# Experts' small products: two groups of four row pairs in every expert instead of three groups

## The chip, the cores and the metric

The kernel runs on one core of one Trainium2 chip. The metric is the time of one execution on the device in microseconds (us), the median of several runs. Engines are named as in the profile: PE is TensorE (PEld its weight loads), ACT is ScalarE, DVE is VectorE, POOL is GpSimd, SP is SyncE, and SPq and POOLq are their DMA queues.

## The reference

One step of a two-layer hybrid trunk over a prompt of 128 tokens and a sample of 1024 tokens, model width 1024, all in float32. Each layer ends with an expert-choice SwiGLU block of 16 experts of width 1024, on which the change bears:

```python
def expert_choice_ffn(h, w_router, w_gate, w_up, w_down):
    B, T, D = h.shape
    cap = EC_CAPACITY * T // N_EXPERTS
    aff = jax.nn.softmax(jnp.einsum('btd,de->bte', h, w_router, preferred_element_type=jnp.float32), axis=-1)
    gate, idx = lax.top_k(aff.swapaxes(1, 2), cap)
    xg = jax.vmap(lambda hb, ib: hb[ib])(h, idx)
    a = jnp.einsum('becd,edf->becf', xg, w_gate)
    u = jnp.einsum('becd,edf->becf', xg, w_up)
    y = jnp.einsum('becf,efd->becd', jax.nn.silu(a) * u, w_down) * gate[..., None].astype(h.dtype)
    return jax.vmap(lambda yb, ib: jnp.zeros((T, D), yb.dtype).at[ib.reshape(-1)].add(yb.reshape(-1, D)))(y, idx)
```

Each expert takes 128 rows of the sample and 16 rows of the prompt. Prompt and sample use the same weights.

## The kernel before, in words

A layer's expert block is `experts` (line 1756 on). Five instruction streams, one for each engine, run side by side and meet at semaphores; the order within each is written out by hand.

The weights come in **chunks** of 128 rows x 1024 columns (512 KB): eight gate chunks (G0 to G7, by k), eight up chunks (U0 to U7) and eight down chunks (D0 to D7) for each expert. `weight_order` (line 1503) lists them: G0, U0, G1, U1, ... G7, U7 of expert e, then D0 to D7 of expert e-1, then the next expert. A chunk n lives in tile n mod 14 of `ffn_w` (`raw_rows`, `RAW_ROOM = 14`).

- SyncE (line 1809 on) loads chunk n when the small products of chunk n-14 are finished:

```python
if n >= RAW_ROOM:
    sp.wait_ge(small_done, 4 * (small[order[n - RAW_ROOM]] + 1))
    sp.dma_start(raw_rows(wall, n), weight_rows(io, l, *chunk)).then_inc(w_in[n % RAW_ROOM], 16)
```

- ScalarE (line 1993) rounds each raw chunk to `w_high`, and VectorE (line 2069) takes the rest as `w_low`; there are `CUT_ROOM = 8` tiles of each, so these two run at most eight chunks ahead of TensorE.
- TensorE multiplies each chunk in `big` (line 1897): three passes (high x high, low x high, high x low) in two halves of 512 columns, into the banks G, U or Y, for the 128 sample rows.
- The 16 prompt rows are multiplied in `small_rows` (line 1919) from the raw chunk itself, without rounding: four products of 16 rows side by side in four column strips of the array, for each k. Of gate and up these are two strips each. Each product counts one on `small_done`, which is what releases the raw tiles.

Where the small products stand in TensorE's order (`k` is the row pair, G and U of one k):

- expert 0: a group for k 0 to 3 after pair 5, and a group for k 4 to 7 after pair 7
- experts 1 to 15: a group for k 0 and 1 after pair 3, a group for k 2 and 3 after pair 5, and a group for k 4 to 7 after pair 7
- the down chunks of expert e-1: a group for k 0 to 3 after D5 and one for k 4 to 7 after D7

In between TensorE also turns things by transposes: h of the expert before after pairs 0 and 1, its prompt part after pair 2, and the gathered tokens of expert e+1 after pairs 4 and 6 (`turn_tokens`). VectorE scales the turned tokens (`set_tokens`, line 2021; the first half behind G6 and the second behind D0), ScalarE rounds them behind D1 (`round_tokens`, line 1985), VectorE cuts them behind D2 (line 2034). Behind D4 ScalarE does the SiLU (lines 1967 to 1972) and VectorE the products with up (`multiply`, lines 2040 and 2044), ahead of D5. GpSimd gathers the tokens of a later expert (line 1816) after `turn_tokens` has freed their buffer, and adds the results back (line 1832).

Of the kernel before, what the change touches and what calls it, by code (L numbers as in the profile page):

```python
# [1516 lines left out]
def raw_rows(wall, n):  # L1517
    return wall[:, (n % RAW_ROOM) * D:(n % RAW_ROOM + 1) * D]
# [237 lines left out]
def experts(nc, io, keep, l, wall):  # L1756
# [7 lines left out]
    with Stage(nc, f"moe{l}") as s:  # L1764
# [86 lines left out]
        def _(pe):  # L1851
            def turn_tokens(e, i):
                if e and i:
                    pe.wait_ge(x_set, NF * e + i)
                elif i == 0:
                    pe.wait_ge(xg_in[e % 2], 16 * (e // 2 + 1))
                    if e >= 2:
                        pe.wait_ge(hpT_done, e - 1)
                    elif e:
                        pe.wait_ge(xp_set, 4)  # L1860
                for k in range(4 * i, 4 * i + 4):
                    mm = nc.tensor.transpose(turned(k, e), xg[e % 2][:, k * P:(k + 1) * P], keep.ident[:])  # L1862
                mm.then_inc(x_turned, 1)

            def turn_prompts(n):
                g, i = divmod(n, 2)
                if n == 0:
                    pe.wait_ge(xgp_in, 16 * (E // PG))
                    pe.wait_ge(x_set, NF)
                else:  # L1870
                    pe.wait_ge(xp_set, n)
                for k in range(4 * i, 4 * i + 4):
                    mm = nc.tensor.transpose(turned(k), xgp[g][:, k * P:(k + 1) * P], keep.ident[:])
                mm.then_inc(xp_turned, 1)

            def turn_h(e, half):
                pe.wait_ge(h_done, e + 1)
                if half:
                    pe.wait_ge(hT_cut, 2 * e + 1)
                for f in range(4):  # L1880
                    mm = nc.tensor.transpose(turn_bank[:, f * P:(f + 1) * P], h[:, (4 * half + f) * P:(4 * half + f + 1) * P], keep.ident[:])
                mm.then_inc(h_turned, 1)

            def turn_hp(e):
                pe.wait_ge(hp_done, e + 1)
                pe.wait_ge(hT_cut, 2 * e + 2)
                for f in range(4):
                    mm = nc.tensor.transpose(turn_bank[:, f * 64:f * 64 + 48], hp[64:112, f * P:(f + 1) * P], keep.ident[64:112, 64:112])
                mm.then_inc(hp_turned, 1)

            def big(bank, stat, e, m, k):
                n = place[e, m, k]
                pe.wait_ge(w_cut, n + 1)
                cut = (w_high[n % CUT_ROOM], w_low[n % CUT_ROOM])
                for i, (a, b) in enumerate(((0, 0), (0, 1), (1, 0))):
                    for half in range(2):
                        mm = nc.tensor.matmul(bank[:, half, :], stat[a][:, k, :], cut[b][:, half * BANK:(half + 1) * BANK],  # L1897
                                              start=k == 0 and i == 0, stop=k == KD - 1 and i == 2)
                mm.then_inc(big_done, 1)

            def small_rows(e, ks, down):
                if not down and ks[0] == 0:
                    pe.wait_ge(xp_set, 4)
                    if e >= 2:
                        pe.wait_ge(yp_done, e - 1)
                if down and ks[0] == 0:
                    pe.wait_ge(hpT_done, e + 1)
                    pe.wait_ge(hp_done, min(e + 2, E))
                    if e == E - 1:
                        pe.wait_ge(yp_done, E - 1)  # L1910
                for k in ks:
                    for q in range(4):
                        if down:
                            n = place[e, "d", k]
                            out, stat, w = small_bank[32 * q:32 * q + CAP_P, 0:256], hpT[:, k // 4, k % 4, :], raw_rows(wall, n)[:, 256 * q:256 * q + 256]
                        else:
                            n = place[e, "gu"[q // 2], k]
                            out, stat, w = small_bank[32 * q:32 * q + CAP_P, :], xpT[:, k, e // PG, CAP_P * (e % PG):CAP_P * (e % PG + 1)], raw_rows(wall, n)[:, BANK * (q % 2):BANK * (q % 2 + 1)]
                        nc.tensor.matmul(out, stat, w, start=k == 0, stop=k == KD - 1, tile_position=(0, 32 * q)).then_inc(small_done, 1)  # L1919

            def down(e):
                if e:
                    pe.wait_ge(ys_done, e)
                pe.wait_ge(hT_cut, 2 * e + 2)
                for k in range(KD):
                    big(Y, (hT_high, hT_low), e, "d", k)
                    if k == 5:
                        small_rows(e, range(0, 4), True)
                small_rows(e, range(4, KD), True)
# [4 lines left out]
            for e in range(E):  # L1934
                pe.wait_ge(x_cut, e + 1)
                if e:
                    pe.wait_ge(h_done, e)
                for k in range(KD):
                    big(G, (xT_high[e % 2], xT_low[e % 2]), e, "g", k)
                    big(U, (xT_high[e % 2], xT_low[e % 2]), e, "u", k)  # L1940
                    if e and k < 2:
                        turn_h(e - 1, k)
                    if e and k == 2:
                        turn_hp(e - 1)
                    if e == 0 and k < 4:
                        turn_prompts(k)
                    if e + 1 < E and k in (4, 6):
                        turn_tokens(e + 1, (k - 4) // 2)
                    if k == 3 and e:
                        small_rows(e, range(0, 2), False)  # L1950
                    if k == 5:
                        small_rows(e, range(2 if e else 0, 4), False)
                small_rows(e, range(4, KD), False)
                if e:
                    down(e - 1)
# [1044 lines left out]
```

## Time and profile before

| What | Value |
|---|---|
| median of 3 runs | 4338.5 us (4337.12 to 4351.47) |
| the profiled execution | 4344.62 us |
| its span, first to last instruction | 4342.8 us |
| TensorE busy over the span | 3623.0 us (83%) |
| VectorE / ScalarE / GpSimd busy | 2370.0 / 1644.5 / 606.4 us |
| mean granted TensorE clock | 0.906 |
| gate and up small products, line 1919 | 2048 records, 237.9 us busy |

The two expert blocks lie at about 1280 to 2080 us and 3490 to 4310 us of the span. Matmuls overlap one another in the records, so the step between two of them is read from their starts, not from their durations. A matmul on plain float32 shows as two records, so a group of 8 small products is "x16" in the timeline and one of 16 is "x32". In a timeline the value in square brackets is the engine's idle time before the row and what ended it.

### The profile page before, as it was taken

The numbers are of one execution on the slowest core, as the hardware profiler recorded it, in microseconds if no ns is written. First come the engines' busy times: TensorE is split into PE (matmuls) and PEld (weight loads), VectorE is DVE, ScalarE is ACT, GpSimd is POOL, SyncE is SP. The second block draws the span as 40 slices with busy tenths as digits, with TensorE's granted clock in tenths as the row PEclk, the third lists the DMA queues.
The fourth block names the chain that finished last, engine by engine and source line by source line (L and its number), as shares of the span: only waits on it lengthen the run. The fifth ranks groups of instructions, "written<-read, shape, count | busy, mean of one in ns | idle before, by whom it ended". The sixth has DMA issues, their size and how long they took to land. (4 is left out here: it accounts for less than half of the span.)

```text
span 4342.8 us, 55242 instructions
## 1 busy us (share of the span) xinstructions
PE 3623.0 (83%) x21964; PEld 2647.4 (61%) x21964; DVE 2370.0 (55%) x3534; ACT 1644.5 (38%) x2480; POOL 606.4 (14%) x472
## 2 busy tenths in 40 slices
PE   3997869797839999999599978419996669999995
PEld 2994524343726666666499956319995446666663
DVE  3233351233477778787412444454555568787874
ACT  2114520000215656565211156524433136565653
POOL 2003110110100001000200000015651000010000
PEclk7998879898969999999799989759997879999997
DMA  4219521411536887887443120352325338878885
GB/s 159 84 61 288 172 73 73 164 53 49 177 147 235 293 296 274 290 291 255 122 118 102 68 89 14 106 148 71 96 71 195 141 142 293 296 274 289 295 284 193
DMA packets 363509, 742.56 MB, mean 171 GB/s; under 512 B 98664, under 2 KB 204279, under 8 KB 362152
## 3 DMA queue, kind: packets, MB, share of 16 engines
q1 hardware_dynamic: 343914, 682.21, 44.9%
q0 software_dynamic: 16720, 56.41, 5.3%
q8 instruction: 175, 2.87, 0.3%
q10 hardware_dynamic: 2618, 0.40, 0.1%
q14 instruction: 82, 0.67, 0.0%
HBM read 633.47 MB, written 106.10 MB: 170 GB/s over the span
## 5 line engine op out<-in xcount | busy, mean ns | idle before, releaser
L2069 DVE TENSOR_TENSOR moe_w_low<-ffn_w,moe_w_high 128x1024 fp32r<-128x1024 f32 x768 | 899.2, 1220 | 97.5 <-ACT moe_w_high L1993 85.3
L1993 ACT ACTIVATE moe_w_high<-ffn_w 128x1024 fp32r<-128x1024 f32 x768 | 778.2, 1053 | 317.0 <-DMA ffn_w<-moe_w_gate 139.3
L1919 PE MATMUL moe_small<-ffn_w,moe_xpT 128*16 128x512 f32 x2048 | 237.9, 594 | 0.0
L1897 PE MATMUL moe_G<-moe_w_high,moe_xT_high 128*128 128x512 f32 x512 | 187.0, 447 | 23.6 <-issue 12.1
L297 PE MATMUL proj_mm<-proj_hT_low,proj_w_high 128*128 128x384 f32 x576 | 193.2, 335 | 0.0
L297 PE MATMUL proj_mm<-proj_hT_high,proj_w_low 128*128 128x384 f32 x576 | 193.1, 335 | 0.0
L297 PE MATMUL proj_mm<-proj_hT_high,proj_w_high 128*128 128x384 f32 x576 | 193.1, 335 | 0.0
L2595 PE MATMUL gdnc_a<-gdnc_T,gdnc_kg 128*128 128x64 f32 (+1 forms) x864 | 102.1, 267 | 89.0 <-ACT gdnc_T L2645 86.8
L297 PE MATMUL proj_mm<-proj_w_high,proj_hT_low 128*128 128x416 f32 (+1 forms) x504 | 176.0, 349 | 0.0
L297 PE MATMUL proj_mm<-proj_w_high,proj_hT_high 128*128 128x416 f32 (+1 forms) x504 | 175.6, 348 | 0.0
L297 PE MATMUL proj_mm<-proj_w_low,proj_hT_high 128*128 128x416 f32 (+1 forms) x504 | 174.8, 347 | 0.0
L1832 POOL DMA_INDIRECT scratch_x<-moe_ys,keep_slot_s x32 | 50.5, 1579 | 877.1 <-DVE moe_ys L2061 877.1
L500 DVE CAST proj_w_high<-proj_w_raw 128x768 fp32r<-128x768 f32 (+1 forms) x60 | 35.0, 583 | 252.1 <-PE proj_mm L297 207.5
L1897 PE MATMUL moe_Y<-moe_w_high,moe_hT_high 128*128 128x512 f32 x512 | 169.8, 413 | 0.0
L1897 PE MATMUL moe_U<-moe_w_high,moe_xT_high 128*128 128x512 f32 x512 | 162.8, 399 | 0.2 <-DVE moe_w_low L2069 0.2
L1897 PE MATMUL moe_G<-moe_w_low,moe_xT_high 128*128 128x512 f32 x512 | 162.8, 399 | 0.0
L1897 PE MATMUL moe_Y<-moe_w_low,moe_hT_high 128*128 128x512 f32 x512 | 162.6, 399 | 0.0
L1897 PE MATMUL moe_Y<-moe_w_high,moe_hT_low 128*128 128x512 f32 x512 | 162.5, 399 | 0.0
L1897 PE MATMUL moe_G<-moe_w_high,moe_xT_low 128*128 128x512 f32 x512 | 162.0, 398 | 0.0
L1897 PE MATMUL moe_U<-moe_w_low,moe_xT_high 128*128 128x512 f32 x512 | 161.7, 397 | 0.0
L1897 PE MATMUL moe_U<-moe_w_high,moe_xT_low 128*128 128x512 f32 x512 | 161.4, 396 | 0.0
L2021 DVE TENSOR_SCALAR moe_xT<-moe_turn,keep_coef 128x128 f32<-128x128 f32 x248 | 84.8, 405 | 125.8 <-PE moe_turn L1862 125.8
(460 smaller groups left out, 7421.9 us busy)
## 6 DMA issues: line engine op xcount, KB each, us to landing
ffn_w<-moe_w_gate SPq DMA_DIRECT2D x256, 512.0 KB, 6.4
ffn_w<-moe_w_up SPq DMA_DIRECT2D x256, 512.0 KB, 7.2
ffn_w<-moe_w_down SPq DMA_DIRECT2D x256, 512.0 KB, 5.6
attnrun_m_w<-w_ada SPq DMA_DIRECT2D x40, 1024.0 KB, 10.7
scratch_conv<-proj_zf POOLq DMA_DIRECT2D x24, 512.0 KB, 2.9
scratch_tm<-proj_tm SPq DMA_DIRECT2D x45, 208.0 KB, 1.9
proj_w_raw<-even_w_in SPq DMA_DIRECT2D x24, 384.0 KB, 4.0
scratch_spec<-filt_res SPq DMA_DIRECT2D x36, 256.0 KB, 2.1
```

The costliest lines, as they stand in the source:

```text
L297: mm = nc.tensor.matmul(out, lhs(a, k), rhs(b, k), start=n == 0, stop=n == len(passes) - 1)
L500: nc.vector.tensor_copy(high, raw).then_inc(w_up, 1)
L1832: nc.gpsimd.indirect_dma_start(out=io["x"][l], out_offset=bass.IndirectOffsetOnAxis(ap=rows, axis=0), in_=src[e % 2][:], in_offset=None, c ...
L1897: mm = nc.tensor.matmul(bank[:, half, :], stat[a][:, k, :], cut[b][:, half * BANK:(half + 1) * BANK], start=k == 0 and i == 0, stop=k == K ...
L1919: nc.tensor.matmul(out, stat, w, start=k == 0, stop=k == KD - 1, tile_position=(0, 32 * q)).then_inc(small_done, 1)
L1993: nc.scalar.activation(w_high[n % CUT_ROOM][:], raw_rows(wall, n), ACT.Copy).then_inc(w_up, 1)
L2021: ins = nc.vector.tensor_scalar(xT[:, k, :], turned(k, e), co[:, 0, k:k + 1], co[:, 1, k:k + 1], ALU.mult, ALU.add)
L2069: nc.vector.tensor_tensor(w_low[n % CUT_ROOM][:], raw_rows(wall, n), w_high[n % CUT_ROOM][:].bitcast(F32), ALU.subtract).then_inc(w_cut, 1)
L2595: mm = nc.tensor.matmul(quad(ba[hg])[later, h, :], kg[n % 3][:, 4 * hg + h, later], earlier(Tm[n % 2][:, 4 * hg + h, :], li, d), start=Tru ...
```

## The change

In experts 1 to 15 of both layers the group for k 0 and 1 after pair 3 goes away, and the group after pair 5 takes k 0 to 3, as in expert 0.

```diff
                     if e + 1 < E and k in (4, 6):
                         turn_tokens(e + 1, (k - 4) // 2)
-                    if k == 3 and e:
-                        small_rows(e, range(0, 2), False)
                     if k == 5:
-                        small_rows(e, range(2 if e else 0, 4), False)
+                        small_rows(e, range(0, 4), False)
                 small_rows(e, range(4, KD), False)
```

On TensorE, behind pair 3 of an expert (`moe_small` is the bank of the small products, `moe_U` and `moe_G` those of up and gate):

```order
 L1897 MATMUL moe_U<-moe_w_low,moe_xT_high 128x512 x2
 L1897 MATMUL moe_U<-moe_w_high,moe_xT_low 128x512 x2
-L1919 MATMUL moe_small<-ffn_w,moe_xpT 16x512 x8
 L1897 MATMUL moe_G<-moe_w_high,moe_xT_high 128x512 x2
 L1897 MATMUL moe_G<-moe_w_low,moe_xT_high 128x512 x2
```

The eight small products of k 0 and 1 are gone from this place; U3 is followed by G4 at once.

On TensorE, behind pair 5 of the same expert:

```order
 L1897 MATMUL moe_U<-moe_w_low,moe_xT_high 128x512 x2
 L1897 MATMUL moe_U<-moe_w_high,moe_xT_low 128x512 x2
-L1919 MATMUL moe_small<-ffn_w,moe_xpT 16x512 x8
+L1919 MATMUL moe_small<-ffn_w,moe_xpT 16x512 x16
 L1897 MATMUL moe_G<-moe_w_high,moe_xT_high 128x512 x2
 L1897 MATMUL moe_G<-moe_w_low,moe_xT_high 128x512 x2
```

They stand here now, ahead of those of k 2 and 3. No other instruction of any engine changes its place, and SyncE's loads and what they wait for are written as before.

## Rows read from the trace of the kernel before

**Rows 1.** Windows in the expert block of layer 0; start:end, length, busy of each engine
```profile
1600.00:1700.00 100.00, 100.00 (x609) 66.98 (x606) 78.70 (x89) 57.28 (x62) 8.55 (x7) 1.00 0.83 288
...
1594.00:1598.00 4.00, 4.00 (x21) 3.11 (x19) 2.53 (x6) 2.59 (x3) 0.00 (x0) 1.00 1.01 408
```

**Rows 2.** Timeline of PE, expert 6 of layer 0; start, length, line, operation
```profile
1589.53 0.63 PE L1897 MATMUL moe_U<-moe_w_high,moe_xT_low 128*128 128x512 f32 x2
1590.09 1.91 PE L1919 MATMUL moe_small<-ffn_w,moe_xpT 128*16 128x512 f32 x16
...
1592.50 0.63 PE L1897 MATMUL moe_G<-moe_w_low,moe_xT_high 128*128 128x512 f32 x2
...
1598.17 1.91 PE L1919 MATMUL moe_small<-ffn_w,moe_xpT 128*16 128x512 f32 x16
...
1605.67 0.63 PE L1897 MATMUL moe_U<-moe_w_high,moe_xT_low 128*128 128x512 f32 x2
1606.23 3.63 PE L1919 MATMUL moe_small<-ffn_w,moe_xpT 128*16 128x512 f32 x32
1609.79 0.73 PE L1897 MATMUL moe_Y<-moe_w_high,moe_hT_high 128*128 128x512 f32 x2
1610.36 0.63 PE L1897 MATMUL moe_Y<-moe_w_low,moe_hT_high 128*128 128x512 f32 x2
```

**Rows 3.** Timeline of PE, expert 0 of layer 1: group, G7, U7, group
```profile
3536.10 3.63 PE L1919 MATMUL moe_small<-ffn_w,moe_xpT 128*16 128x512 f32 x32
...
3543.64 0.73 PE L1897 MATMUL moe_G<-moe_w_high,moe_xT_high 128*128 128x512 f32 x2 [0.47 <-DVE moe_w_low L2069]
...
3545.14 0.63 PE L1897 MATMUL moe_U<-moe_w_high,moe_xT_high 128*128 128x512 f32 x2
...
3546.63 3.63 PE L1919 MATMUL moe_small<-ffn_w,moe_xpT 128*16 128x512 f32 x32
```

**Rows 4.** Timelines of SP, ACT and DVE, the same expert; the loads' landing times
```profile
3537.29 0.35 SPq L1811 DMA_DIRECT2D ffn_w<-moe_w_gate  x1
...
3541.26 1.06 ACT L1993 ACTIVATE moe_w_high<-ffn_w 128x1024 fp32r<-128x1024 f32 x1 [13.69 <-DMA ffn_w<-moe_w_gate]
...
3542.36 3.79 DVE L2069 TENSOR_TENSOR moe_w_low<-ffn_w,moe_w_high 128x1024 fp32r<-128x1024 f32 x3 [5.50 <-ACT moe_w_high L1993]
3546.06 1.36 DVE L2021 TENSOR_SCALAR moe_xT<-moe_turn,keep_coef 128x128 f32<-128x128 f32 x4
...
DMA to landing us min/median/max: 3.4/6.2/12.7
```

**Rows 5.** Timeline of PE, expert 0 of layer 0: its two small groups
```profile
1316.17 3.63 PE L1919 MATMUL moe_small<-ffn_w,moe_xpT 128*16 128x512 f32 x32
...
1327.55 3.63 PE L1919 MATMUL moe_small<-ffn_w,moe_xpT 128*16 128x512 f32 x32
```

**Rows 6.** Timeline of ACT, expert 6 of layer 0: G7, U7, then the tokens
```profile
1594.97 1.06 ACT L1993 ACTIVATE moe_w_high<-ffn_w 128x1024 fp32r<-128x1024 f32 x1 [2.76 <-DMA ffn_w<-moe_w_gate]
1596.24 1.06 ACT L1993 ACTIVATE moe_w_high<-ffn_w 128x1024 fp32r<-128x1024 f32 x1 [0.20 <-DMA ffn_w<-moe_w_up]
...
1604.95 1.06 ACT L1985 ACTIVATE moe_xT_high<-moe_xT 128x1024 fp32r<-128x1024 f32 x1 [5.12 <-DVE moe_xT L2021]
```

**Rows 7.** Timeline of DVE, expert 6 of layer 0: the tokens, and from D5 on
```profile
1603.55 1.37 DVE L2021 TENSOR_SCALAR moe_xT<-moe_turn,keep_coef 128x128 f32<-128x128 f32 x4 [2.17 <-PE moe_turn L1862]
...
1613.51 10.08 DVE L2069 TENSOR_TENSOR moe_w_low<-ffn_w,moe_w_high 128x1024 fp32r<-128x1024 f32 x8
```

**Rows 8.** Timelines of PE and ACT: an early first load, a late second load
```profile
3856.31 1.91 PE L1919 MATMUL moe_small<-ffn_w,moe_xpT 128*16 128x512 f32 x16
3861.06 1.06 ACT L1993 ACTIVATE moe_w_high<-ffn_w 128x1024 fp32r<-128x1024 f32 x1 [2.63 <-DMA ffn_w<-moe_w_gate]
...
1637.91 1.91 PE L1919 MATMUL moe_small<-ffn_w,moe_xpT 128*16 128x512 f32 x16
1646.39 1.06 ACT L1993 ACTIVATE moe_w_high<-ffn_w 128x1024 fp32r<-128x1024 f32 x1 [2.47 <-DMA ffn_w<-moe_w_up]
```

## Prediction

> **What bounds the kernel now.** I read the windows first, then TensorE's timeline inside one expert, then the timelines of SyncE, ScalarE and VectorE beside it. In the expert loop TensorE is busy 100.00 of 100 us at full granted clock, while VectorE has 79 and ScalarE 57 us of work and the DMA engines 83% [rows 1]: the loop ends with TensorE. One expert takes 47.8 us (the small group after k=3 starts at 1590.09 in one expert [rows 2], at 1637.91 in the next [rows 8]). So a slot saved on TensorE is saved in the time, and a wait put into TensorE is paid in full. What the loop hides is the ring of 14 raw row tiles. SyncE loads a tile again only when the small products have read it, so each small group is also what releases loads.
>
> **What is removed.** 30 experts (15 in each of two layers, e of 1 to 15) lose one group of 8 small products; its work moves into the group after k=5. No product, semaphore increment, DMA or cut is added or dropped. The price of a group, from start to start of the pairs around it: U's last pair at 1589.53, G's second pair at 1592.50, 2.97 us for 8 products; for 16 products 1605.67 to 1610.36, 4.69 us [rows 2]. A plain step from pair to pair is 0.467 us (three pairs take 1.50 us in rows 3, the first 0.1 longer after the pause). Before: 2 x 2.97 = 5.94 us. After: one 4.69 and two plain steps, 0.93, 5.62 us. **Saved: 0.32 us per expert, 9.6 us in all.** It is the entry and exit of one group. It is small because the 16 products cost the same wherever they stand.
>
> **What moves later.** The tiles of k=0 and k=1 are now released after k=5, two row pairs later on TensorE. They hold the place of G7 and U7 of the same expert (chunk n goes where n-14 was) and of the first two down chunks. All other releases keep their group. So from group start to the moment TensorE wants G7 there is now little: the rest of the group, k=6, a turn of four transposes. Before, k=4 and k=5 lay between as well.
>
> Expert 0 of each layer already runs the new form, and there the wait shows. Layer 1: group at 3536.10, SyncE issues G7 at 3537.29 (+1.19), ScalarE starts on it at 3541.26 (+5.16), VectorE at 3542.36, TensorE at 3543.64 after 0.47 us idle [rows 3, 4]. From ScalarE's start to TensorE's is 2.38 us. The next small group starts 1.50 + 1.49 us later, at 3546.63. Call x the time from group start to ScalarE's start on G7: the next group then comes at x + 5.37. Without a wait it comes at 9.78: it is 8.06 us in expert 6 (1598.17 to 1606.23) for a group of 8 products [rows 2], and the bigger group puts back TensorE by 4.69 - 2.97 = 1.72. So **the wait is x - 4.41**. Expert 0 gives 10.53 - 9.78 = 0.75 us in layer 1, and 11.38 - 9.78 = 1.60 us in layer 0 [rows 3, 5].
>
> For the other experts x can be read now, at the group after k=3, whose first release is the same G7: 1590.09 to 1594.97, 4.88 us [rows 2, 6]. Over all 30 it runs from 4.75 (3856.31 to 3861.06, [rows 8]) to 5.76, mean 4.98. **The wait on G7: 30 x (4.98 - 4.41) = 17.1 us**, and 0.8 more because the last expert of each layer has no transposes before G7 (0.42 us less cover), 17.9.
>
> U7 follows G7 on ScalarE by 1.27 us (1594.97, 1596.24, [rows 6]); TensorE takes 1.50 us for G7, so as a rule U7 is hidden. In six experts the second load is late: the worst has ScalarE on U7 at 1646.39, 8.48 us after its group at 1637.91 [rows 8], which is 3.54 behind its own G7 and 2.04 more than TensorE covers. The six exceed 1.50 by 0.47, 2.04, 0.44, 1.56, 0.82 and 0.45: **5.8 us**.
>
> **The next one that could be late is D5**, the sixth down chunk. ScalarE and VectorE had slack here: after D1 ScalarE sat 5.12 us waiting for the transposed tokens [rows 6], and now it comes to that point later. VectorE starts on the tokens 4.80 us after x (3546.06 against 3541.26, [rows 4]), ScalarE's rounding follows 1.40 later (1603.55 to 1604.95), VectorE's cut of D5 starts 8.56 after that rounding (1613.51) [rows 6, 7], and TensorE can use a cut 1.28 after its start [rows 3, 4]: x + 16.04. TensorE comes to D5 at x + 2.38 + 1.50 + 1.49 + 3.56 (group, 1606.23 to 1609.79, [rows 2]) + 7.10 (five chunks of 1.40 and 0.10), x + 16.03. It is a tie. The lower bound is nothing; the upper is some 0.5 us, if the gather of tokens for a later expert, one more 512 KB tile that used to run in an empty stretch, now shares the DMA engines with D2 to D5. I take 0.1 us, near the tie that the rows give: **2.8 us** for 28 experts.
>
> **Sum:** 17.9 + 5.8 + 2.8 - 9.6 = +16.9 us. The profiled execution took 4344.62 us (span 4342.8), 6.1 above the median of 4338.5. The difference is put on the median: **4355.4 us**, 0.39% slower. A measurement of this kernel can tell about 0.3% (13 us) from no change.
>
> **Rule against row, 1.** From the issue of G7 to ScalarE's start it takes 3.97 us in layer 1's expert 0 and 3.69 in expert 6 (4.88 less the same 1.19), and the shortest load of the trace took 3.4 us from issue to landing [rows 4, 6]. The Trainium skill (DMA: Bandwidth & Descriptors, "Anatomy of one DMA") fits a DMA, issued by GpSimd, as about 2.0 us plus the bytes over 436 GB/s, an estimate of 3.2 us for 512 KB. By that rule x would be 1.19 + 3.2 = 4.39, the wait on G7 nothing and the time 4329 us. This case's rows are longer, and they decide.
>
> **Rule against row, 2.** Between 1594 and 1598 us the DMA engines were full and moved 408 GB/s [rows 1], or 1.29 us for a tile. The Trainium skill (same page, "Specifications") names a limit of about 358 GB/s from HBM for a core; by that rule a tile would take 1.46 us, an estimate, U7 would still be hidden, and the third chunk and with it D5 would come some 0.4 us later, 11 us more in all. The trace does not show that limit.
>
> **The rivals.**
> *Not slower: the loads come in time.* Break-even is where the wait is worth the group, x = 4.41 + 0.32 = 4.73. The shortest x now is 4.75, so the edge is near. If after the bigger group the loads land as fast as the fastest one of the trace, x = 1.19 + 3.4 = 4.59, the wait is 0.18 and the kernel gains 0.14 x 30 = 4 us: 4334 us. With no wait at all it would gain 9.6 us: 4329. For it: SyncE's queue has been quiet longer by then. Against: it was quiet longer still in expert 0, and x was 5.16 and 5.50 there. Chance 0.15. By the Trainium skill's fit (rule 1) this would be the outcome.
> *All experts behave as expert 0 does.* With 0.75 us each, 22.5 - 9.6 is +13; with 1.60, 48 - 9.6 is +38: 4351 to 4377 us, in the middle +26, 4364. For it: the same form of the program. Against: in layer 0 one odd issue of 1.4 us on SyncE lies in it. Chance 0.17.
> *D5 becomes the bound.* Loads released two pairs later now lie against the gather; if that puts 0.5 to 1 us on D5, 14 to 28 us come on top: 4368 to 4382. For it: the tie. Against: tiles come 1.27 us apart, so D2 lands about x + 5.1, and ScalarE wants it at x + 7.2 (4.80, 1.40 and one rounding). By the Trainium skill's limit (rule 2) this would be the outcome. Chance 0.13.
> *The change does nothing*, because what TensorE loses before G7 it used to lose elsewhere. Rows 1 leave no idle time that could be so given back. Chance 0.03.
>
> **How the numbers follow.** My forecast has 0.52, and reaches by itself from +9 to +25 us (D5 at nothing, fewer or more late second loads); about two thirds of it lie above +13. Slower by over 0.3%: 0.35 of the forecast, 0.13 of the expert-0 case and 0.12 of the D5 case, 0.60. Faster by over 0.3%: the largest gain is 9.6 us, so only scatter gives it, 0.03. The rest, 0.37, is within 0.3%. The range goes from 4336 (the better half of the first rival left out) to 4378, the upper end of the expert-0 case (part of the D5 case left out).
>
> **What would show it.** Right: small groups of 16 products only, 9.8 + 0.5 us apart; in each expert an idle stretch of 0.2 to 0.6 us on TensorE before G7, released by VectorE's cut; an expert of about 48.3 us; ScalarE's wait for G7's load moved behind the group after k=5. Wrong: TensorE still 100% busy and an expert of 47.5 us (rival one), waits before U7 in most experts, or waits before D5 or the third small group (rival three).

## The result, and the profile after

| | before | after |
|---|---|---|
| median of 6 runs | 4343.38 us (4337.12 to 4351.47) | 4376.23 us (4366.96 to 4382.02) |
| ratio to before, 95% interval | | 1.0074 (1.0059 to 1.0089) |
| span of the profiled execution | 4342.8 us | 4380.2 us |

The change costs 32.9 us by the medians, 0.74% (26 to 39 us by the interval). The forecast was +16.9 us: the right sign, half the size, and the time lies just inside the range. 4.9 us of the distance between 4355.4 and 4376.2 come from before itself, whose median went from 4338.5 to 4343.4 with three more runs; 16 us are the change's own.

The page of the profile after, its busy times (before: 3623.0, 2647.4, 2370.0 and 1644.5 us):

```profile
PE 3639.6 (83%) x21964; PEld 2655.7 (61%) x21964; DVE 2371.5 (54%) x3534; ACT 1636.9 (37%) x2480; POOL 617.2 (14%) x472
```

The windows view of twelve experts of layer 0 (start:end, length, busy of PE, PEld, DVE, ACT and POOL, granted clock, DMA share, GB/s):

```profile
1400.00:1980.00 580.00, 571.81 (x3484) 378.01 (x3483) 453.37 (x500) 336.71 (x370) 54.82 (x35) 1.00 0.77 281
```

The same instructions are issued, and TensorE, which was busy for 580.00 of the same 580 us before, now has 8.2 us of idle time in them, at the same full clock. (The ends of matmuls are modelled and reach over their successors, so a wait is longer from start to start than as idle time. The one of 1.06 us below is 1.22: 2.62 from one product to the next, where 1.40 is the usual step. The first step inside a product behind a pause is 0.1 longer too, so the groups around this wait stand 1.33 us further apart.) The view of waits says before what (engine, what waits <- what ended it: us in total, times, longest), after, 1400 to 1980 us:

```profile
PE moe_Y L1897 <- DVE moe_w_low L2067: 4.7, 8, 1.1
PE moe_G L1897 <- DVE moe_w_low L2067: 2.2, 7, 0.5
...
PE moe_U L1897 <- DVE moe_w_low L2067: 0.9, 2, 0.5
```

There are waits before a G and a U chunk, as forecast, but the largest item is before a Y product, that is a down chunk. One expert shows where. TensorE's timeline after, expert 2 of layer 0, from the group of gate and up after pair 5 to the down group:

```profile
1413.55 3.63 PE L1919 MATMUL moe_small<-ffn_w,moe_xpT 128*16 128x512 f32 x32
...
1423.51 3.63 PE L1919 MATMUL moe_small<-ffn_w,moe_xpT 128*16 128x512 f32 x32
1427.07 0.74 PE L1897 MATMUL moe_Y<-moe_w_high,moe_hT_high 128*128 128x512 f32 x2
...
1435.40 0.73 PE L1897 MATMUL moe_Y<-moe_w_high,moe_hT_high 128*128 128x512 f32 x2 [1.06 <-DVE moe_w_low L2067]
```

This is the lone group of 16 products ("x32") where [rows 2] had one of 8. The Y product at 1435.40 is the sixth since 1427.07: D5.

The distance between neighbouring groups, read from the starts in TensorE's timeline and summed over the 30 experts, splits the loss. Apart from the moved products and the group saved, nothing else in the cycle changed: the distance from the down group after D5 to the one after D7 is 4.84 us in both.

| stretch of an expert's cycle | before | after | difference |
|---|---|---|---|
| group after pair 5 to group after pair 7 | 241.2 us (8.07 each) | 315.5 us (9.96 to 13.55) | 292.6 without a wait, so **22.9 us lost** at G7 and U7 |
| group after pair 7 to group after D5 | 364.4 us (12.15 each) | 380.1 us (12.15 to 13.49) | **15.7 us of waits** before D5 |
| the whole cycle of an expert, without waits | 47.80 us each | 47.49 us each | **-9.3 us** |

The 292.6 us are 28 x 9.78 and 2 x 9.36 for the last expert of each layer: the 8.07 and 7.64 us of before and 1.72 for the bigger group, as in the prediction. Together +29.3 us. Of the 37.4 us between the two spans 6.8 lie ahead of the first small group of layer 0 (1316.17 before, 1322.94 after), which the change does not touch; 0.7 lie in the two experts 0 and 0.6 between the two expert blocks, and the sum explains the rest.

Not all of the 22.9 us is waiting. In expert 8 of layer 1 G7 came so late that TensorE stood idle for 2.1 us, and behind that pause the granted clock was halved for 3.4 us, from 3950.2 on (TensorE's row, then the windows view):

```profile
3948.93 0.74 PE L1897 MATMUL moe_G<-moe_w_high,moe_xT_high 128*128 128x512 f32 x2 [2.10 <-DVE moe_w_low L2067]
```

```profile
3951.00:3953.00 2.00, 2.00 (x6) 1.34 (x4) 2.00 (x6) 0.70 (x2) 0.00 (x0) 0.50 1.00 412
```

G7 and U7 took 4.39 us there from G7's start to the next group (3948.93 to 3953.32), where 2.99 is usual: 1.4 us of the 22.9 are work at the lower clock, 1.2 instead of 2.4 GHz.

### The profile page after: what moved, and what is told of

Read it like the earlier page. It is cut to its first block and busy times, and to the rows that moved or that the text cites. A ratio compares the mean times of both kernels' runs of the same rounds, so it can differ in the third digit from the quotient of the medians.

```text
span 4380.2 us, 55242 instructions
## 1 busy us (share of the span) xinstructions
PE 3639.6 (83%) x21964; PEld 2655.7 (61%) x21964; DVE 2371.5 (54%) x3534; ACT 1636.9 (37%) x2480; POOL 617.2 (14%) x472
## 5 line engine op out<-in xcount | busy, mean ns | idle before, releaser
L2593 PEld LDWEIGHTS gdnc_a<-gdnc_T,gdnc_kg 128*128 128x128 f32 (+1 forms) x864 | 92.9, 182 | 95.1 <-issue 93.7
```

The source lines that it names most:

```text
L2593: mm = nc.tensor.matmul(quad(ba[hg])[later, h, :], kg[n % 3][:, 4 * hg + h, later], earlier(Tm[n % 2][:, 4 * hg + h, :], li, d), start=Tru ...
```

## The experiments

All ratios are to the kernel before, run beside it on the same chip; the medians of before were 4351.4 us in both sets, 8 us above the one of the table above, so only ratios are compared across sets.

**The first group after pair 4, or after pair 3.** Two groups as in the change, only earlier; the edit is to the changed kernel. The theory was that the late release of the raw tiles is the loss, the rival that the group of 16 itself is.

```diff
-                    if k == 5:
+                    if k == (4 if e else 5):
                         small_rows(e, range(0, 4), False)
```

The other version has 3 in place of 4.

> Two groups as in the change, but in experts 1 to 15 the first one, all four row pairs, stands after pair 4 (expert 0 as before). Theory (late release): the loss of the change is not in the bigger group but in when it releases the raw tiles. The group now comes a pair (2.8 us) earlier, so G7, D0 and the rest land at least 2.8 us before the time at which they were late by 0.2 to 1.1 us. The waits before G7 and U7 (22.7 us in the changed kernel, against none before) and before D5 (15.7 us) go to 0 to 3 us, the price of one group stays saved, 9 us: 0.990 to 0.993 of the changed kernel, and 0.2% under the kernel before. Rival (size): a group of 16 small products is itself the harm, for example since it keeps the DMA queue from being fed evenly: then the time stays near the changed kernel's.

> Two groups, the first one (four row pairs) after pair 3, in the place where the kernel before had its first group of two; expert 0 as before. Theory (late release): G7 is released when it was in the kernel before and the down chunks D2 to D5 earlier than ever; no wait before G7, U7 or D5, TensorE without idle time between 1400 and 1980 us, each expert about 47.5 us, some 9 us (0.2%) under the kernel before and the same as the version with the group after pair 4. Rival (size): slower than the kernel before, as the changed kernel is.

Measured: after pair 4, 0.9975 (0.9965 to 0.9985); after pair 3, 0.9970 (0.9959 to 0.9981). Every distance between groups is the same in all experts again, 47.48 and 47.49 us for an expert's cycle against 47.80 before. Windows of 1400 to 1980 us, after pair 4:

```profile
1400.00:1980.00 580.00, 580.00 (x3568) 389.88 (x3567) 464.28 (x514) 346.65 (x378) 52.41 (x35) 1.00 0.80 286
```

No idle time is left. The group of 16 does no harm by itself; the whole loss comes from where it stands. Moving it one pair, 2.8 us, turns +0.74% into -0.25%.

**SiLU and product behind D5.** Again an edit to the changed kernel. It looks at the wait that the forecast had put at 2.8 us.

```diff
-                if m == "d" and k == 4 and e + 1 < E:
+                if m == "d" and k == 5 and e + 1 < E:
                     silu(e + 1)
...
-                if m == "d" and k == 4 and e + 1 < E:
+                if m == "d" and k == 5 and e + 1 < E:
                     multiply(e + 1)
```

> The changed kernel with the SiLU on ScalarE and the products with up on VectorE behind D5 instead of ahead of it. Theory (chain): the wait before D5, 15.7 us over 30 experts, is that of a chain which starts with the load of D0, runs over VectorE's tokens, ScalarE's rounding, D2 to D4 and the SiLU and product (1.97 us on VectorE), and ends with D5's cut. Without the product ahead of it D5 is ready 1.97 us earlier, so the wait before D5 goes to 0 to 2 us in all, the small group after D5 may wait a little (0 to 4 us in all), and the time is 12 to 16 us under the changed kernel, while the waits before G7 and U7 stay at about 23 us. Rival (transfer): D5's own load is late, then the wait before D5 stays.

Measured: 1.0038 (1.0024 to 1.0051), against 1.0074 of the change: 0.36% or some 15.6 us won, and the two intervals do not meet. From the group after pair 7 to that after D5 it is 364.5 us in all, the 364.4 of before: no wait at D5, and none at the small group behind it. The waits before G7 and U7 stay, 22.1 us (314.7 less 292.6). In one expert with a late D0, ScalarE's timeline and VectorE's:

```profile
1511.12 1.06 ACT L1991 ACTIVATE moe_w_high<-ffn_w 128x1024 fp32r<-128x1024 f32 x1 [1.40 <-DMA ffn_w<-moe_w_down]
```

```profile
1519.07 3.49 DVE L2067 TENSOR_TENSOR moe_w_low<-ffn_w,moe_w_high 128x1024 fp32r<-128x1024 f32 x3
1522.48 1.21 DVE L2038 TENSOR_TENSOR moe_h<-moe_sg,moe_U 128x1024 f32<-128x1024 f32 x1
```

The three cuts at 1519.07 are D3, D4 and D5: D5 no longer stands behind the product. So D5's own load was not late; its place in VectorE's order was.

**The gather moved.** The other reason that could make D5 late: the gather of tokens beside the down loads. In the changed kernel it goes behind the add-backs.

```diff
-                if e + 4 < E:
-                    pool.wait_ge(x_turned, NF * (e + 3))
-                    fetch(e + 4)
                 pool.wait_ge(ys_done, e + 1)
                 pool.wait_ge(yp_done, e + 1)
                 add_back(e)
+                if e + 4 < E:
+                    pool.wait_ge(x_turned, NF * (e + 3))
+                    fetch(e + 4)
```

> The changed kernel with the gather of a later expert's tokens behind the add-back instead of behind the second turn of tokens, so that it no longer shares the DMA engines with D1 to D5. Theory (chain, without the gather): nothing changes, within 3 us of the changed kernel, the wait before D5 stays at about 16 us. Rival (contention, the reason that the prediction gave for D5's upper bound): the wait before D5 goes, 12 to 16 us are won.

Measured: 1.0058 (1.0045 to 1.0071). GpSimd's timeline shows the gather where it was sent, behind the add-backs, which start at 1440.49 and 1442.37:

```profile
1444.08 1.02 POOL L1816 DMA_INDIRECT moe_xg<-scratch_xn,keep_slot_s  x1 [0.30 <-issue]
```

and an expert with no gather near it still waits at D5 (ScalarE's D0, then TensorE's D5):

```profile
1414.49 1.06 ACT L1991 ACTIVATE moe_w_high<-ffn_w 128x1024 fp32r<-128x1024 f32 x1 [1.52 <-DMA ffn_w<-moe_w_down]
```

```profile
1427.96 0.73 PE L1897 MATMUL moe_Y<-moe_w_high,moe_hT_high 128*128 128x512 f32 x2 [1.10 <-DVE moe_w_low L2067]
```

The waits before D5 sum to 14.7 us here (379.1 less 364.4), against 15.7. That is 1 us less, where the rival asks for 12 to 16. The ratio's interval overlaps that of the change; whether the rest of its 0.16% is a gain elsewhere is not settled.

**The price of a group.** The kernel before with one group more, and nothing released later; the edit is to the kernel before.

```diff
+                    if k == 6 and e:
+                        small_rows(e, range(4, 6), False)
-                small_rows(e, range(4, KD), False)
+                small_rows(e, range(6 if e else 4, KD), False)
```

> The kernel before with one group more: in experts 1 to 15 the last group of 16 small products (rows 4 to 7) is split in two of 8, after pair 6 and after pair 7. No release comes later than before, some come earlier. It measures the price of a group by itself. Theory: 0.30 us an expert, 30 experts, 9 us more than before (1.002), TensorE still without idle time between 1400 and 1980 us. Rival: the earlier release of four tiles helps elsewhere and the time stays, or the price of a group depends on what stands around it and is over 0.5 us (15 us and more).

Measured: 1.0023 (1.0011 to 1.0035), 10 us. From the group after pair 3 to that after D5 the timeline has 28.62 us (8.07 + 20.55) against 28.29 before (8.07 + 8.07 + 12.15): 0.33 us for a group (9.9 us in 30 experts), with TensorE busy for 580.00 of 580 us.

**Only row pair 0 early.** Three groups: 4 products after pair 3, 12 after pair 5. The edit is shown against the kernel before.

```diff
                     if k == 3 and e:
-                        small_rows(e, range(0, 2), False)
+                        small_rows(e, range(0, 1), False)
                     if k == 5:
-                        small_rows(e, range(2 if e else 0, 4), False)
+                        small_rows(e, range(1 if e else 0, 4), False)
```

> Three groups again, but only the small products of row pair 0 (4 of them) stand after pair 3; those of pairs 1 to 3 stand after pair 5. So G7 and U7 are released as in the kernel before, D0 to D5 at pair 5. Theory (late release of G7, U7 and D0): the wait before G7 and U7 (22.7 us) goes; D0 is now the first release of the group after pair 5 and lands about 5 us after its start instead of 7.6 to 8.5, so the wait before D5 goes too; the price of a group is back: the time of the kernel before, within 4 us (1.000). Rival: what counts is how many tiles are released late, then half or more of the loss (15 us and more) stays.

Measured: 0.9999 (0.9989 to 1.0009), no idle time on TensorE in 580 us, and the worst D5 late by 0.16 us. TensorE's timeline has the groups of 4, 12 and 16 products ("x8" at 1600.78, "x24" at 1607.98 and "x32" at 1616.92 in one expert).

Six of the eight tiles are released as late as in the change, at no cost. So the loss hangs on the first two releases alone, which free the tiles of G7 and U7, and on D0 standing third in the same row.

**A version that beats both.** The first group after pair 4 in all experts, and one group for the down chunks; the edit is to the changed kernel.

```diff
-                    if k == 5:
+                    if k == 4:
                         small_rows(e, range(0, 4), False)
...
                 for k in range(KD):
                     big(Y, (hT_high, hT_low), e, "d", k)
-                    if k == 5:
-                        small_rows(e, range(0, 4), True)
-                small_rows(e, range(4, KD), True)
+                small_rows(e, range(0, KD), True)
```

> A version that should beat both: the first group of four row pairs after pair 4 in every expert, expert 0 too, and the small products of the down chunks in one group of 32 after D7 instead of 16 after D5 and 16 after D7. Theory: a group is worth 0.30 us wherever no load becomes late. Against the kernel before 9 us for gate and up, 9 to 10 us for down (32 experts), about 2 to 4 us of waits in expert 0: 18 to 23 us less, 0.995 to 0.996. The first tile that the late down group releases is wanted as G3 of the next expert 12.9 us after the group's start and would be ready after 7.4, so no wait there. Rival: all eight releases in one bunch come too late for G3 to U6, the loads follow each other at 1.27 to 1.30 us and a late one in a bunch (up to 2.5 us) is no longer covered: waits appear before G3 to G6 and the time is that of the version with the group after pair 4, or above it.

Measured: 4323.85 us, ratio 0.9938 (0.9925 to 0.9952), 27 us under the kernel before. That is more than the 18 to 23 us expected, though the interval reaches up to 0.9952, 21 us; the 0.64 us an expert of the timeline give 19. The two experts 0, from their G0 to the next, take 81.4 us together against 87.4 before; but the two versions above, which leave expert 0 as it was in the kernel before, have 84.8 and 87.1 there, so a part of those 6 us may be scatter. TensorE's timeline has three groups to an expert, 47.16 us from one expert to the next:

```profile
1593.66 3.63 PE L1919 MATMUL moe_small<-ffn_w,moe_xpT 128*16 128x512 f32 x32
...
1621.19 3.65 PE L1919 MATMUL moe_small<-ffn_w,moe_hpT 128*16 128x256 f32 x64
1640.82 3.63 PE L1919 MATMUL moe_small<-ffn_w,moe_xpT 128*16 128x512 f32 x32
```

In the window of 580 us TensorE is never idle: the loads of G3 to U6, released in one bunch after D7, are in time.

## Why the prediction was half right

**The bound.** Right. A slot saved and a wait put in on TensorE both show in the time: the distances explain 29.3 us, and the medians say 32.9 with an interval of 26 to 39.

**What is saved,** forecast 9.6 us: 9.3 us in the change, 9.9 by the price of 0.33 us, 0.25 and 0.30% in the versions without waits.

**The waits before G7 and U7,** forecast 17.9 + 5.8 = 23.7 us: 22.9 us. G7's part was right: the mean x of 4.98 us is the same in the profile after, some 18 us of waits, though one G7 came very late (x = 6.78). U7 was late in four experts instead of six, some 3.5 us instead of 5.8, and the 1.4 us of the lower clock, which the forecast did not have, make up for part of it. So the method, to read the delay of a load where it is still hidden and set it against the shorter cover, held; that the sum agrees within 1 us is in part luck. The late U7 have a sign on SyncE: it took 0.76 to 1.27 us to issue that load in three of the four, and 0.84 to 1.42 in the three latest of the six before, where 0.43 is usual. Expert 0, already in the new form, gave the right direction, but its two values, 0.75 and 1.60 us, would have given 22 to 48 us.

**The wait before D5,** forecast 2.8 us: 15.7 us. This is the step that failed. "It is a tie" was worked out from x with VectorE's tokens at x + 4.80, as layer 1's expert 0 has it, where the third load follows G7 by 2.56 us, and it holds only where D0 does so too. I had looked for late loads among the second ones and stopped there; the third one was in the same timeline. From ScalarE's rows of the kernel before, D0 starts 3.14 us after G7 in the mean, more than 2.8 in 20 of 30 experts, and the excess over 2.54 us sums to 17.9 us. This expert of the kernel before (ScalarE: G7, then D0; U7 at 1787.75 was on time) shows it, hidden then because ScalarE had still to wait until 1796.18 for the turned tokens:

```profile
1786.31 1.06 ACT L1993 ACTIVATE moe_w_high<-ffn_w 128x1024 fp32r<-128x1024 f32 x1 [2.88 <-DMA ffn_w<-moe_w_gate]
...
1790.36 1.06 ACT L1993 ACTIVATE moe_w_high<-ffn_w 128x1024 fp32r<-128x1024 f32 x1 [1.54 <-DMA ffn_w<-moe_w_down]
```

With a tie, each late D0 goes into the time whole, unless a late G7 or U7 has already held TensorE back. The chain itself was right to 0.02 us. After, in the expert of 1413.55 us, ScalarE and VectorE:

```profile
1421.93 1.06 ACT L1991 ACTIVATE moe_w_high<-ffn_w 128x1024 fp32r<-128x1024 f32 x1 [1.45 <-DMA ffn_w<-moe_w_down]
...
1425.57 1.06 ACT L1983 ACTIVATE moe_xT_high<-moe_xT 128x1024 fp32r<-128x1024 f32 x1 [1.30 <-DVE moe_xT L2019]
```

```profile
1432.15 1.22 DVE L2038 TENSOR_TENSOR moe_h<-moe_sg,moe_U 128x1024 f32<-128x1024 f32 x1
...
1434.12 2.36 DVE L2067 TENSOR_TENSOR moe_w_low<-ffn_w,moe_w_high 128x1024 fp32r<-128x1024 f32 x2
```

The rounding of the tokens at 1425.57 plus the 9.84 us of the forecast is 1435.41, and D5 starts at 1435.40. It is the same in the others: in 27 of the 28 experts D5 starts 13.46 to 13.49 us after ScalarE starts D0 (13.47 here), and in the 28th, the one with the halved clock, the chain was ready before TensorE came. In the expert of 1512.00 us D0 was on time (7.73 after the group), and TensorE has no idle time at D5. The runs with the product behind D5 and with the gather moved leave this chain as the cause and rule out contention with the gather, which stood behind the upper bound. That upper bound, 0.5 us an expert, is about what was measured (0.56), but for a reason that was not the true one.

**The rivals.** "Not slower" is out: x did not shorten, and the Trainium skill's fit (DMA: Bandwidth & Descriptors, "Anatomy of one DMA"), made for a DMA that GpSimd issues, by which a 512 KB load would be an estimated 3.2 us, would have had no wait here; the waits came. "D5 becomes the bound" came true near the low end of its price, 0.56 us in each of 28 experts where it had 0.5 to 1, and by another way than the gather. The Trainium skill's limit of about 358 GB/s (same page, "Specifications") is not what did it: on-time tiles still followed each other at 1.27 us, 413 GB/s. "As expert 0" was near in time by accident: expert 0 has no down chunks behind G7 and says nothing of D5. It was this rival that put the upper end of the range at 4378 us; the forecast's own reach ended at +25 us, and the measured 32.9 lies beyond it. That the time fell inside the range, 1.8 us below its end, is owed to that, and is luck.

## What to carry to other kernels

Where the work that frees a buffer is postponed to save an overhead, list all the loads that it releases, each with its own spread of landing times and its own first user, and follow each chain to the next one that is just in time; the late ones of a hidden load are in the trace before the change. Where two placements save the same, take the earlier one: a pair of 2.8 us was the difference between losing 0.74% and winning 0.25%. And a chain that comes out as a tie is to be priced by the spread of its inputs, never at nothing.

## What was not expected of the hardware

The third tile that SyncE's queue loads after a pause is often late. ScalarE starts D0 over 2.8 us after G7 in 20 of 30 experts, both before and after, in 14 and 16 of them with U7 on time; two tiles behind each other take 2.54, and the third is up to 1.5 us later than that. Its issue was not late: it stands 2.05 us after the group's start in all of those 14 and in 15 of the 16. Where D0 is late with U7 on time, the DMA engines move less in the sixth microsecond after the group's start. The windows of one such expert of the changed kernel, then of one with both on time:

```profile
1418.55:1419.55 1.00, 1.00 (x6) 0.78 (x5) 0.31 (x1) 0.78 (x2) 0.00 (x0) 1.00 0.74 258
1517.00:1518.00 1.00, 1.00 (x6) 0.77 (x6) 0.00 (x0) 0.81 (x1) 0.00 (x0) 1.00 0.99 356
```

The DMA engines move 258 instead of 356 GB/s, with only the weight queue at work. The late one of the pair is an extreme: the mean of the 16 late experts is 299 GB/s, and that of the 10 with both on time 363; before the change the means are 343 and 370. It is not the gather: with it moved D0 is late in 20 of 30 experts still. What it is stays open; no run looked for it.
